# Weights loaded in two parts per chunk into six staging buffers, and the groups' sums collected two strips before their scattering

## What is computed

```python
N_EXPERTS, N_GROUPS, GROUP_SIZE, TOP_K, D_EXPERT = 16, 4, 4, 2, 512

def grouped_moe(h, router_w, router_bias, w_gate, w_up, w_down):
    scores = jax.nn.sigmoid(jnp.einsum('nd,de->ne', h, router_w))
    biased = (scores + router_bias).reshape(n, N_GROUPS, GROUP_SIZE)
    group_sel = jnp.argmax(jnp.sum(lax.top_k(biased, TOP_K)[0], axis=-1), axis=-1)
    ...
    for e in range(N_EXPERTS):
        a = jax.nn.silu(h @ w_gate[e]) * (h @ w_up[e])
        y = y + dense_gates[:, e:e + 1] * (a @ w_down[e])
    return y

def reference(...):
    x = first_block(...)     # 2 layers: attention mixer, layer norm, grouped_moe, layer norm
    return second_block(...) # 2 layers: gated FFN, SSD or attention mixer, cross attention, gated FFN
```

## Time and profile before

| | us |
|---|---|
| median of 3 runs | 2499.16 (2486.32 to 2501.43) |
| the profiled execution, timed | 2494.47 |
| its span in the profile | 2492.7 |
| mean granted TensorE clock | 0.929 |
| PE busy | 2202.5 (88%) |
| DVE busy | 1543.3 (62%) |
| ACT busy | 1214.8 (49%) |
| HBM read over the span | 443.80 MB, 178 GB/s |

### The profile page before, as it was taken

How to read it: one execution, slowest core, us unless ns; L and a number is a source line. 1 busy time by engine, 2 the same in 40 slices (tenths; PEclk the granted TensorE clock), 3 DMA queues, 4 the chain that set the end, 5 groups by cost and what they waited for, 6 DMA issues and landing times.

```text
span 2492.7 us, 31042 instructions
## 1 busy us (share of the span) xinstructions
PE 2202.5 (88%) x12158; PEld 1905.0 (76%) x12158; DVE 1543.3 (62%) x2122; ACT 1214.8 (49%) x1958; POOL 76.6 (3%) x79
## 2 busy tenths in 40 slices
PE   4975999997985999989999797889999997888999
PEld 4764877775764877767999776769989995777998
DVE  5456888886545888876555747555555555365554
ACT  3342777763442777664444443534444445343443
POOL 0001000000001000000000002000000001000000
PEclk9897999998896999999999899889999998598999
DMA  5212798982212888873455342324554544031553
GB/s 205 70 68 87 278 338 337 351 316 87 86 68 70 316 333 322 345 304 138 169 186 187 119 152 85 129 77 178 188 193 153 190 182 170 1 137 68 186 186 119
DMA packets 64015, 447.01 MB, mean 179 GB/s; under 512 B 7632, under 2 KB 8400, under 8 KB 11088
## 3 DMA queue, kind: packets, MB, share of 16 engines
q1 hardware_dynamic: 63856, 444.88, 48.3%
HBM read 443.80 MB, written 1.05 MB: 178 GB/s over the span
## 4 chain that ended last, share of the span: by engine, by line
PE 47%; DVE 5%; ACT 2%; issue 1%; POOL 0%; DVEq 0%; POOLq 0%; ACTq 0%
PE bank L619 7%; PE bank L620 7%; PE bank L621 7%; PE bank L587 4%; PE bank L588 4%; PE bank L589 4%; PE bank L1007 3%; PE bank L1008 3%; PE bank L1009 3%; PE bank L661 2%; PE bank L871 1%; ACT scr L744 1%; DVE lo L550 1%; PE bank L2190 1%; DVE scr L2734 1%
## 5 line engine op out<-in xcount | busy, mean ns | idle before, releaser
L550 DVE TENSOR_TENSOR lo<-stage,hi 128x1024 fp32r<-128x1024 f32 x832 | 969.4, 1207 | 332.6 <-ACT hi L538 282.6
L538 ACT ACTIVATE hi<-stage 128x1024 fp32r<-128x1024 f32 x832 | 825.0, 1041 | 331.0 <-PE bank L589 127.8
L619 PE MATMUL bank<-thi,hi 128*128 128x256 f32 x1504 | 428.6, 285 | 3.4 <-DVE lo L550 2.0
L620 PE MATMUL bank<-tlo,hi 128*128 128x256 f32 x1504 | 427.6, 284 | 0.0
L621 PE MATMUL bank<-thi,lo 128*128 128x256 f32 x1504 | 427.5, 284 | 0.0
L619 PEld LDWEIGHTS bank<-thi,hi 128*128 128x128 f32 x1504 | 291.1, 194 | 5.5 <-issue 3.9
L620 PEld LDWEIGHTS bank<-tlo,hi 128*128 128x128 f32 x1504 | 290.9, 193 | 1.4
L621 PEld LDWEIGHTS bank<-thi,lo 128*128 128x128 f32 x1504 | 290.7, 193 | 0.0
L587 PE MATMUL bank<-hi,thi 128*128 128x512 f32 (+2 forms) x656 | 262.1, 400 | 23.2 <-ACT scr L2608 8.2
L588 PE MATMUL bank<-lo,thi 128*128 128x512 f32 (+2 forms) x656 | 256.5, 391 | 0.0
L589 PE MATMUL bank<-hi,tlo 128*128 128x512 f32 (+2 forms) x656 | 255.9, 390 | 0.0
(11 more groups left out here) (319 smaller groups left out, 2890.1 us busy)
## 6 DMA issues: line engine op xcount, KB each, us to landing
stage<-in_exp SPq DMA_DIRECT2D x192, 1024.0 KB, 4.9
stage<-in_ffn SPq DMA_DIRECT2D x132, 1024.0 KB, 4.8
stage<-in_wi_a SPq DMA_DIRECT2D x8, 1024.0 KB, 4.9
stage<-in_wi_b SPq DMA_DIRECT2D x8, 1024.0 KB, 4.8
stage<-in_mem_wkv SPq DMA_DIRECT2D x8, 1024.0 KB, 5.2
stage<-in_xwq SPq DMA_DIRECT2D x8, 1024.0 KB, 4.8
stage<-in_xwo SPq DMA_DIRECT2D x8, 1024.0 KB, 4.7
stage<-in_ssd_xbc SPq DMA_DIRECT2D x6, 1024.0 KB, 4.8
```

Of the source, the lines that this page charges most:

```text
L538: a.activation(self.hi[i % NR][:, x:y], self.stage[i % NS][:, x:y], ACT.Copy).then_inc(*c.tick(("hi", i, p), sem="hi"))
L550: v.tensor_tensor(self.lo[i % NR][:, x:y], self.stage[i % NS][:, x:y], self.hi[i % NR][:, x:y].bitcast(F32), ALU.subtract).then_inc(*c.tic ...
L619: t.matmul(out, hi[:, ws], self.thi[:, xs], start=(k == 0), stop=False)
L620: t.matmul(out, hi[:, ws], self.tlo[:, xs], start=False, stop=False)
```

## The change

Two edits. First, there are six staging buffers of 1024 columns instead of three of 2048. `load` issues two DMA transfers per chunk, for its left and its right half, each with a semaphore of its own, and each waits only for the `hi` and `lo` of the same half three chunks before. The splits wait for their own half alone. Second, `collect(g - 1)` moves on ACT and DVE from `at == 4` to `at == 2`. The two sends and the adds stay. PE's program is unchanged.

```diff
-        self.stage = [sb(f"stage{i}", CW) for i in range(NS)]
+        self.stage = [sb(f"stage{i}", CW // 2) for i in range(2 * NS)]
...
     def load(self, s, c, i):
         name, at, n = self.chunks[i]
         src = self.d[name][at:at + 128 * n].rearrange("(p c) -> p c", p=128)
-        if i >= NS:
-            for w in c.need(("hi", i - NS, 1), ("lo", i - NS, 1)):
-                s.wait_ge(*w)
-        s.dma_start(self.stage[i % NS][:, :n], src).then_inc(*c.tick(("ld", i), sem=f"ld{i % NS}", by=16))
+        for p, (x, y) in enumerate(((0, n // 2), (n // 2, n))):
+            if i >= NS:
+                for w in c.need(("hi", i - NS, p), ("lo", i - NS, p)):
+                    s.wait_ge(*w)
+            b = (2 * i + p) % (2 * NS)
+            s.dma_start(self.stage[b][:, :y - x], src[:, x:y]).then_inc(*c.tick(("ld", i, p), sem=f"ld{b}", by=16))
...
-            for w in c.need(("ld", i), ("used", i - NR) if i >= NR else None):
+            for w in c.need(("ld", i, p), ("used", i - NR) if i >= NR else None):
                 a.wait_ge(*w)
-            a.activation(self.hi[i % NR][:, x:y], self.stage[i % NS][:, x:y], ACT.Copy).then_inc(
+            a.activation(self.hi[i % NR][:, x:y], self.stage[(2 * i + p) % (2 * NS)][:, :y - x], ACT.Copy).then_inc(
...
@@ compact_act
-            if g and at == 4:
+            if g and at == 2:
                 collect(g - 1)
@@ compact_dve
+            if g and at == 2:
+                collect(g - 1)
             if g and at == 4:
-                collect(g - 1)
                 send(g - 1, 0)
```

More of the change, by code:

```diff
@@ L470, in __init__ @@
         self.bank = [ctx.enter_context(nc.psum_tensor(f"bank{i}", [128, 512], F32)) for i in range(8)]
-        names = ("pe", "act", "dve", "pool", "hi", "lo", "used", *(f"ld{i}" for i in range(NS)),
+        names = ("pe", "act", "dve", "pool", "hi", "lo", "used", *(f"ld{i}" for i in range(2 * NS)),
                  "d_const", "d_x", "d_rw", "d_row", "d_ln", "d_late", "d_out")
@@ L547, in split_dve @@
         for p, (x, y) in enumerate(((0, n // 2), (n // 2, n))):
-            for w in c.need(("ld", i), ("hi", i, p), ("used", i - NR) if i >= NR else None):
+            for w in c.need(("ld", i, p), ("hi", i, p), ("used", i - NR) if i >= NR else None):
                 v.wait_ge(*w)
-            v.tensor_tensor(self.lo[i % NR][:, x:y], self.stage[i % NS][:, x:y],
+            v.tensor_tensor(self.lo[i % NR][:, x:y], self.stage[(2 * i + p) % (2 * NS)][:, :y - x],
                             self.hi[i % NR][:, x:y].bitcast(F32), ALU.subtract).then_inc(
```

## The result

| | before | after |
|---|---|---|
| median | 2500.3 us (4 runs beside after, 2486.32 to 2514.61) | 2462.49 us (4 runs, 2454.82 to 2464.74) |
| ratio, 95% interval | | 0.985 [0.981, 0.989] |
| profiled execution, its span | 2494.5, 2492.7 | 2454.8, 2452.9 |
| 62 pairs of the experts | 570.1 | 537.0 |
| of these, six with the first send | 89.87 | 56.28 |

The forecast was 2457 (2446 to 2486). The kernel became 1.5% faster, inside the range. The rows on pairs are windows from transposes to transposes (L1885 after, L1883 before), summed.

A forecast was written before the change was run, and what follows sets the result against it. PE was taken as the bound, in the experts with DMA and DVE close behind. From the profiled 2494.5: -33.6 (collection at the send) +2 (its new place) -5 (halves) -1 (start) = 2456.9, so 2457 us, range 2446 to 2486.

The forecast's parts named there:

- The collection at the send: Six expert pairs that collect and send fall from 89.9 to 56.3 us, wait and clock loss together: 33.6 us removed.
- The collection at its new place: In the pairs that now collect, splits queue behind the collection: 0.3 us each taken, +2 us; bounds nothing to 8.
- a debt of DVE's queue: At the new place DVE has 9.1 us of work in 8.46; the debt of 0.7 is repaid in the next pairs.
- Halves, 5 us: Half loads shorten each expert buffer's round to 5.5 us, removing PE's waits on `hi`: 5 us gained, bounds 0 and 6.6.
- The landing: A 512 KB half load in the experts lands 3.3 us after issue, 3.3 to 3.5 expected in the profile.
- The program's start, 1 us: DVE's first four halves of `lo` end at about 19.1 to 19.3 instead of 20.31, gaining 1 us on the path.
- A: Rival: the moved collection delays the splits, 2463 us, or 2470 to 2480 with a fallen clock; latter or C's mild form 0.18.
- B: Rival: PE's wait at or behind the send only changes its name, to the adds or `alo`; 2488 or more, chance 0.10.
- C: Rival: slower loads bound the experts; mild 2472 us (0.18 shared with fallen-clock A), proper 2528, above 2510 chance 0.10.
- bound of 1.41 us a half: Six half transfers per 8.46 us pair allow 1.41 us each; 1.2 to 1.4 was taken, so no cost.
- DMA share of 0.99: DMA engines shown busy for 0.99 of the undisturbed expert pair; part was held to be start-up and not use.
- 2.0 us fixed plus bytes over 436 GB/s: Skill's cost of one DMA: 3.2 us for a half, 6.4 instead of 4.4 for a chunk if run singly.

The follow-up runs named there:

- half the bytes: Kernel before with only the collection moved to `at == 2`, loading only the left 1024 columns of each expert chunk: 2448.06 us, ratio 0.980 to before.
- halves as blocks: Changed kernel with each half of a chunk stored as one block in HBM, rows without gaps: 2439.84 us, ratio 0.978 to before.
- after again: The changed kernel itself, unaltered, measured and profiled a second time on another kernel pair's chip: 2465.38 us, ratio 0.989 to before.
- collection alone: Kernel before with only the collection moved to `at == 2`, keeping three whole staging buffers: 2475.76 us, ratio 0.991 to before.
- blocks, late release: Changed kernel, halves stored as blocks, both halves' loads issued only after the second half's `lo` three chunks before: 2463.81 us, ratio 0.988 to before.
- halves, late release: Changed kernel, but both halves' loads issued only after the second half's `lo` three chunks before: 2506.45 us, ratio 1.002 to before.
- the halves alone: Changed kernel with the collection put back to `at == 4`, keeping the six half buffers: 2487.92 us, ratio 0.996 to before.
- the collection at `at == 1`: Changed kernel with the collection one chunk earlier still, `at == 1` for `at == 2`: 2479.8 us, ratio 0.993 to before.
- quarters: Changed kernel with each half loaded by two DMAs of 512 columns, 256 KB each: 2465.24 us, ratio 0.984 to before.

## Why the prediction was right, and where it was not

**The collection at the send, 33.6 us.** Right to the decimal: 89.87 became 56.28. The choice of the next pair as the price, wait and clock together, was what made it so; the granted clock in the six windows is 1.00.

**The collection at its new place, 2 us.** The size is right by luck, 52.61 - 50.76 = 1.9 (3.3 in the second profile; over the 51.35 that these pairs took before it is 1.3 and 2.7). The reason is not. I put it down to a debt of DVE's queue, and with quick loads the same code takes 50.76, which is nothing.

**Halves, 5 us. This is the step that failed.** The 50 pairs, which hold this term and the last one, went from 424.0 to 423.9; without the six pairs of the collection it is 372.6 to 371.3, so the term measured 1.3, and 0.6 of that went back in the pairs with the second send. In the second profile of the same kernel the 50 pairs took 431.8. Two things were wrong in it:

- The landing. I took the 3.3 us of the `ukv` loads of 512 KB for a half in the experts. It is 5.8. The earlier trace rows also had two loads of 512 KB that took 7.6 and 8.4 us, and I used those for their spacing only. The round trip of a buffer is then not 3.3 + 1.0 + 1.2 = 5.5, far from any limit, but 8.0 in a pair of 8.46.
- What it is set against. I reckoned what PE loses to loads from the trace of before, where six stalls, such as the 3.37 us of the earlier trace rows, give the loads time to catch up. Without them whole loads cost 18.6 us more in the 50 pairs (442.6), and this is what the halves prevent. By the pairs of the profiles, edit 2 is worth 12.8 us by itself, and edit 1 another 20.3 on top of it (12.8 by the second profile of after). By the medians it is 21.7 and another 10 to 13.

That the sum came out is in part luck. By edits, the prediction gave edit 2 31.6 us and edit 1 5 in the pairs, where the profiles show 12.8 and 20.3: too much for the one and too little for the other, and the sum of 36.6 stands against 33.1. In the second profile, 25.6, they cancel less well. The forecast of 2457 us is 5.6 under the median of 2462.49, and the nearness of the profiled execution (2454.8) owes 5.5 us to the start, below. The round trips, made from each page's landing and the 1.0, 1.2 or 2.36 of the splits, put the kernels nearly in order:

| kernel | round trip | mean of the 50 pairs |
|---|---|---|
| half the bytes | 3.8 + 3.4 = 7.2 | 8.35 |
| halves as blocks | 5.3 + 2.2 = 7.5 | 8.35 |
| after | 5.8 + 2.2 = 8.0 | 8.48 |
| after again | 6.0 + 2.2 = 8.2 | 8.64 |
| collection alone | 4.9 + 3.4 = 8.3 | 8.85 |
| blocks, late release | 5.0 + 3.4 = 8.4 | 8.55 |
| halves, late release | 5.9 + 3.4 = 9.3 | 9.20 |

The fifth and sixth stand the other way round, so it is a guide and no law (a median landing hides the late ones, and a half may be split while the other is still on its way). Up to 7.5 no pair waits; at 9.3 the pair takes the round trip.

**The program's start, 1 us.** DVE's four halves of `lo` begin and end earlier than in the earlier trace rows, as the timeline of after shows:

```profile
13.52 5.07 DVE L552 TENSOR_TENSOR lo<-stage,hi 128x1024 fp32r<-128x1024 f32 x4 [13.52 <-ACT hi L540]
...
18.50 1.28 DVE L713 BATCH_NORM_STATS2 st<-scr 128x6 f32<-128x512 f32 x2
```

They end at 18.59 against 20.31, 1.7 us; PE's wait for x fell from 31.3 to 29.6, the same. But this wait differs as much between profiles of the same start code: 29.6, 30.3, 30.6 and 31.1 with after's (after, the halves alone, after again, the collection at `at == 1`), 31.3, 31.3 and 30.4 with before's (before, the collection alone, half the bytes). The means, 30.4 and 31.0, are 0.6 apart, so the term is not shown to be more than that.

The first pair of the experts begins 5.5 us earlier, and this can't be given to the change: the same kernels with after's start code gave 261.5, 257.3, 262.2 and 274.8, and those with before's 267.0, 274.9 and 268.2. What it goes with is the granted clock in the first 250 us, 0.90, 0.92, 0.90 and 0.86 in the former and 0.89, 0.86 and 0.87 in the latter; where it is 0.86 the two codes stand at 274.8 and 274.9. So the span's -39.8 (33.1 in the pairs, 5.5 ahead of them, 1.2 elsewhere) is no proof of more than the first part.

**The rivals.** A did not happen: the new place costs 2 us, from the loads, and nothing where they are quick. The collection at `at == 1` shows what splits held behind a collection cost, though there it is a wait of ACT that holds them. B did not happen: no wait stands at the send. C was nearer than I gave it credit for. Its bound of 1.41 us a half holds (six halves per 8.46 us are moved in after), but I had given the DMA share of 0.99 away as start-up. In half the bytes it is 0.57 at the same time per pair, so it was mostly use. That halves could take longer than whole loads by their pitch, which C named as 3% in rate, is shown by the late release with and without blocks: 579.2 against 541.4, 7%. What kept C away from the change is that the left half is asked for earlier, by the 1.2 us of a `lo`.

One comparison of the prediction was loose. The 2.0 us fixed plus bytes over 436 GB/s of the Trainium skill (DMA: Bandwidth & Descriptors, section Anatomy of one DMA) are stated for transfers that GpSimd issues, while SP issues those here. And the 4.9 us that the prediction took for a load by itself is the median of all expert loads. No term of the sum rests on this comparison.

What stays open is how the chip comes by the cost of the pitch. The runs show that it is not the number of transfers (quarters) nor, by themselves, rows of 4 KB (blocks of 4 KB rows are quick), and that the packets of the DMA engines take longer; which part of the path takes longer for rows that are 8 KB apart was not measured.

## What to carry to other kernels

A stall of the engine that sets the pace is also slack for whatever feeds it: before taking it away, compute the feeder's round trip against the stall-free pace, not against the waits that the trace shows today. Take the landing of a load from the busy stretch where it will run, not from a lone load of the same size. And where a load is cut in two by columns, store each part as a block of its own: here that was worth another 23 to 26 us.

## What the hardware showed that I had not expected

- Reading halves with rows of 4 KB at a pitch of 8 KB is slower than reading the same bytes as blocks: 4.7 against 4.1 us to landing in the FFN, 5.8 against 5.3 in the experts, where nothing else in the program differed.
- Cutting each half again into two transfers of 256 KB cost nothing (2465.24 against 2465.38 us), with several under way at a time.
- With a pitch of 8 KB the DMA engines moved 331 GB/s while they were busy for 0.96 of the time, as blocks 356 at the same share (both with the late release).
- The first 260 us of the program differ by up to 17 us between profiles with the same code there (257.3 to 274.8 at the experts' first transposes), and the granted clock in the first 250 us goes with it. The halves alone, then the collection at `at == 1`:

```profile
0.00:250.00 250.00, 175.96 (x938) 145.34 (x939) 142.59 (x288) 96.20 (x212) 16.58 (x18) 0.92 0.31 107
...
0.00:250.00 250.00, 180.53 (x881) 149.18 (x881) 131.81 (x258) 89.69 (x202) 16.59 (x18) 0.86 0.31 107
```

Why the clock differs between executions of the same start code is not shown.
